# A transformer layer with retrieved experts: 344 dense tokens in place of 352, three slot groups for the gathered ones, and a gate table read four blocks at a time

## The reference

```
q = (x @ w_query) per head, two halves          # 8 heads
s = q . sub_keys                                # 2 x 128 scores per head
top 16 of each half, then top 16 of the 256 sums -> 16 experts per head, 128 per token
g = softmax(top scores)                         # one gate per expert
hid = gelu(x . u_tab[expert])                   # u_tab, v_tab: 16384 x 2048
out = sum over experts of g * hid * v_tab[expert]
```

## Time and profile before

| | before |
|---|---|
| median of 3 runs | 3497.88 us |
| the profiled execution's own time | 3498.18 us |
| its span | 3496.4 us |
| TensorE busy | 3327.0 us, 95% |
| VectorE busy | 2788.3 us, 80% |
| ScalarE busy | 998.9 us, 29% |
| GpSimd busy | 1131.7 us, 32% |
| moved by DMA | 897.01 MB, mean 257 GB/s |

### The profile page before, as it was taken

How to read it: one execution, slowest core, us unless ns; L and a number is a source line. 1 busy time by engine, 2 the same in 40 slices (tenths; PEclk the granted TensorE clock), 3 DMA queues, 4 the chain that set the end, 5 groups by cost and what they waited for, 6 DMA issues and landing times.

```text
span 3496.4 us, 48435 instructions
## 1 busy us (share of the span) xinstructions
PE 3327.0 (95%) x19321; PEld 3047.2 (87%) x19321; DVE 2788.3 (80%) x3985; ACT 998.9 (29%) x1240; POOL 1131.7 (32%) x568
## 2 busy tenths in 40 slices
PE   7999999996898999889999999999999999999996
PEld 2688888886896447889999999999999999999996
DVE  6888888888676668977887787787678878878776
ACT  2322222223223002433333323323323322332222
POOL 2443333333350577002332322233123323333220
PEclk9999999998998999999999999999999999999998
DMA  9644444443556212458989889988788988999895
GB/s 401 240 160 165 160 156 159 159 165 133 206 178 258 105 60 73 171 204 299 336 337 347 329 334 340 337 330 335 261 321 326 339 329 324 341 336 328 329 352 201
DMA packets 199241, 897.01 MB, mean 257 GB/s; under 512 B 81893, under 2 KB 82702, under 8 KB 108430
## 3 DMA queue, kind: packets, MB, share of 16 engines
q1 hardware_dynamic: 152974, 558.82, 43.9%
q0 software_dynamic: 46080, 335.56, 25.0%
HBM read 858.03 MB, written 35.21 MB: 255 GB/s over the span
## 4 chain that ended last, share of the span: by engine, by line
PE 79%; DVE 12%; issue 4%; DMA 3%; POOL 2%; ACT 1%; SPq 0%; DVEq 0%; ACTq 0%; POOLq 0%
PE ps_all L987 17%; PE ps_all L1047 9%; PE ps_all L1053 9%; PE ps_all L1048 9%; PE ps_all L994 8%; PE ps_all L952 6%; PE ps_all L714 5%; PE ps_all L716 5%; PE ps_all L715 5%; DVE sb_hot L1897 2%; PE ps_all L660 1%; DVE sb_hot L1893 1%; DVE sb_tops L1626 1%; DVE sb_arena L1630 1%; DMA sb_raw_ring<-in_v_t 1%
## 5 line engine op out<-in xcount | busy, mean ns | idle before, releaser
L1342 ACT ACTIVATE sb_raw_hi<-sb_raw_ring 128x2048 fp32r<-128x2048 f32 x256 | 490.8, 1918 | 1215.8 <-DMA sb_raw_ring<-in_v_t 535.9
L1047 PE MATMUL ps_all<-sb_w_hi,sb_raw_hi 128*128 128x352 f32 x2048 | 658.1, 324 | 20.3 <-DVE sb_w_lo L1916 13.6
L987 PE MATMUL ps_all<-sb_h_hi,sb_raw_hi 128*128 128x352 f32 x2048 | 662.9, 326 | 5.9 <-issue 5.9
L1821 DVE TENSOR_TENSOR sb_raw_lo<-sb_raw_ring,sb_raw_hi 128x2048 fp32r<-128x2048 f32 x256 | 586.5, 2291 | 98.7 <-ACT sb_raw_hi L1342 98.4
L987 PE MATMUL ps_all<-sb_h_lo,sb_raw_hi 128*128 128x352 f32 x2048 | 661.0, 324 | 0.0
L1048 PE MATMUL ps_all<-sb_w_lo,sb_raw_hi 128*128 128x352 f32 x2048 | 656.6, 322 | 0.0
L2086 POOL DMA_INDIRECT sb_gather_ring<-in_u_tab,sb_kept x160 | 267.6, 1673 | 829.8 <-DVE sb_kept L1936 623.6
L2086 POOL DMA_INDIRECT sb_gather_ring<-in_v_tab,sb_kept x160 | 281.4, 1759 | 670.3 <-DVE sb_acc_a L1948 467.5
L1047 PEld LDWEIGHTS ps_all<-sb_w_hi,sb_raw_hi 128*128 128x128 f32 x2048 | 386.1, 189 | 21.9 <-issue 20.2
L2012 POOL TENSOR_TENSOR sb_w_low<-sb_w_raw,sb_w_high 128x2048 fp32r<-128x2048 f32 (+1 forms) x64 | 265.4, 4146 | 427.2 <-ACT sb_w_high L1153 427.2
L987 PEld LDWEIGHTS ps_all<-sb_h_hi,sb_raw_hi 128*128 128x128 f32 x2048 | 387.8, 189 | 6.7 <-issue 6.7
(11 more groups left out here) (270 smaller groups left out, 5608.3 us busy)
## 6 DMA issues: line engine op xcount, KB each, us to landing
sb_raw_ring<-in_u_t SPq DMA_DIRECT2D x128, 1024.0 KB
sb_raw_ring<-in_v_t SPq DMA_DIRECT2D x128, 1024.0 KB
sb_arena<-in_ada_wt SPq DMA_DIRECT2D x96, 512.0 KB, 4.3
sb_w_raw<-in_w_t SPq DMA_DIRECT2D x32, 1024.0 KB, 5.0
sb_w_raw<-in_w_v SPq DMA_DIRECT2D x32, 768.0 KB, 4.1
sb_g_ring<-table_scratch SPq DMA_DIRECT2D x64, 352.0 KB
sb_arena<-in_ada_w SPq DMA_DIRECT2D x10, 2048.0 KB, 11.8
table_scratch<-sb_stage SPq DMA_DIRECT2D x7, 2816.0 KB, 8.7
```

The costliest lines, as they stand in the source:

```text
L987: last = mm(acc, raw_hi[:, r[0], kk * P:(kk + 1) * P], part[:, kk, :], start=i == 0, stop=False)
L1047: mm(accs[c], v, w_hi[:, slots[e], :], start=e == 0, stop=False)
L1342: acti(raw_hi[:, k % 2, :], raw_ring[:, k % RAW, :], ACT.Copy).then_inc(S["un_hi"], 1)
L1821: vec.tensor_tensor(raw_lo[:, k % RAW, :], raw_ring[:, k % RAW, :], raw_hi[:, k % 2, :].bitcast(f32), ALU.subtract)\
```

## The change

The dense tokens become 344 (XT = 40), cut into 8 stages of 43. A stage has ten groups of 4 tokens and one of 3. The gate table is read four blocks at a time (`QUAD`), each row piece 172 numbers long. The last 40 tokens stand three times over the partitions (120 rows used), in groups of 43, 43 and 42 slots; their 43 transfers still fetch 128 rows, the last 8 by an index cleared to 0, and VectorE works on 120. `DOTS` is 171 per table. The third part of `y_t` has 88 tokens; its banks are cleared by a matmul with zeros, the tokens come in by matmuls with the unit matrix, and the three groups by `pick_x`, all added up in the same banks. The small tiles that are kept over the stage are placed elsewhere.

```diff
-XT = 32
+XT = 40
 XG = P // XT
+XP = XG * XT
 ND = T - P - XT
-XSLOTS = SLOTS // XG
+XSLOTS = -(-SLOTS // XG)
-NGROUP = ND // GROUP
-STAGE = 44
+STAGE = 43
-PER_STAGE = STAGE // GROUP
+PER_STAGE = -(-STAGE // GROUP)
+NGROUP = NSTAGE * PER_STAGE
+QUAD = 4
 def slot_at(n):
-    m, j = n // 5, n % 5
-    return (True, 4 * m + j) if j < 4 else (False, SLOTS + m)
+    m, j = n // 4, n % 4
+    return (True, 3 * m + j) if j < 3 and n < DOTS - 1 else (False, SLOTS + m)
+def group_at(n):
+    c = n % PER_STAGE * GROUP
+    return n // PER_STAGE, c, min(GROUP, STAGE - c)
...
-        g_ring = placed("g_ring", at, [P, 2, NSTAGE, 2 * STAGE])
+        g_ring = placed("g_ring", at, [P, 2, NSTAGE, QUAD * STAGE])
...
+            def g_load(q):
+                if QUAD * q in QUARTERS:
+                    sp.wait_ge(S[f"g_quarter{QUARTERS.index(QUAD * q)}"], 16)
+                wait(sp, "gated", QUAD * (q - 1))
+                sp.dma_start(g_ring[:, q % 2, :, :], g_d[:, :, QUAD * q * STAGE:QUAD * (q + 1) * STAGE].rearrange("n j c -> j n c"))\
+                    .then_inc(S[f"g_in{q % 2}"], 16)
...
-            for p in range(2):
-                g_load(p)
+            g_load(0)
+            g_load(1)
             stage_store(NSTAGE - 1, (1, 2, 3))
             g_load(2)
             next_load(EARLY - 2)
-            for p in range(3, 5):
-                g_load(p)
             for k in range(EARLY - 1, UNITS):
                 next_load(k)
-                if k in (14, 17, 19, 22):
-                    g_load((14, 17, 19, 22).index(k) + 5)
-                if kind == "up" and n >= EARLY and n % 2 and n + 3 < NKEYS:
-                    g_load((n + 3) // 2)
+                if k in (EARLY - 1, EARLY + 5):
+                    g_load((EARLY - 1, EARLY + 5).index(k) + 3)
+                if kind == "up" and n >= EARLY and n % QUAD == QUAD - 1 and n + 1 + QUAD < NKEYS:
+                    g_load((n + 1) // QUAD + 1)
...
                 if t == 2:
                     pe.wait_ge(S["zs"], 2)
                     pe.wait_ge(S["sq_done"], 2)
                     pe.wait_ge(S["pick_x"], 1)
+                    zeros, any_rows = pick_x[:, 0:1].to_broadcast([P, P]), ident[:, :].unsqueeze(1).to_broadcast([P, 4, P])
+                    for b in range(4):
+                        mm(psum[:, y0 + b * NB:y0 + (b + 1) * NB], zeros, any_rows, start=True, stop=False)
+                        for kk in range(4 * b, 4 * b + 4):
+                            mm(psum[0:n, y0 + kk * P:y0 + (kk + 1) * P], y_t[:, kk, at:at + n], ident[:, :], start=False, stop=False)
                     pe.wait_ge(S["gr_used"], 2 * DOTS)
                     for b in range(4):
-                        last = mm(psum[n:P, y0 + b * NB:y0 + (b + 1) * NB], pick_x, acc_x[:, b * NB:(b + 1) * NB], start=True, stop=True)
+                        last = mm(psum[:, y0 + b * NB:y0 + (b + 1) * NB], pick_x[0:XP, :], acc_x[0:XP, b * NB:(b + 1) * NB], start=False, stop=True)
...
+            link(vec.tensor_scalar(gates_x, iota[:, 0:XSLOTS], 0.0, None, ALU.mult))
+            vec.tensor_copy(eidx_x, gates_x)
             vec.tensor_copy(eidx_a, pair_id[:, 0, :])
             vec.tensor_copy(eidx_last, pair_id[:, 1, :]).then_inc(S["g_fin"], 1)
...
+            link(vec.tensor_scalar(pick_x, ident[:, :], 0.0, None, ALU.mult))
+            vec.tensor_reduce(pick_x[:, P - XT:P], ident[:, 0:XP].rearrange("p (a j) -> p j a", a=XG), axis=AX, op=ALU.add)\
+                .then_inc(S["pick_x"], 1)
```

More of the change, by code:

```diff
@@ L249, in build_program @@
         hid_all = take(DOTS)
-        pick_x = take(XT)
-        at = SM + D
         raw_hi = rounded("raw_hi", at, [P, 2, D])
@@ L257, in build_program @@
         stage = [placed(f"stage{n}", a, [P, NKEYS, STAGE]) for n, a in enumerate((at, M0))]
-        take = carver(placed("route_b", at, [P, 7 * D // 2]))
+        pick_x = placed("pick_x", at + 2 * (S8 + 2) * ND, [P, P])[:, :]
+        take = carver(placed("route_b", at, [P, 2 * (S8 + 2) * ND]))
         qt_sb = take(2 * T).rearrange("p (m t) -> p m t", m=2)
@@ L605, in _ @@
             for a in range(XG):
-                part, cols_ = slice(a * XT, (a + 1) * XT), slice(a * XSLOTS, (a + 1) * XSLOTS)
-                sp.dma_start(eidx_x[part, :], eidx_last[P - XT:P, cols_]).then_inc(S["xe_in"], 16)
-                sp.dma_start(gates_x[part, :], gates[P - XT:P, NT - 1, cols_]).then_inc(S["xe_in"], 16)
+                first, end = a * XSLOTS, min((a + 1) * XSLOTS, SLOTS)
+                part, place, slots = slice(a * XT, (a + 1) * XT), slice(0, end - first), slice(first, end)
+                sp.dma_start(eidx_x[part, place], eidx_last[P - XT:P, slots]).then_inc(S["xe_in"], 16)
+                sp.dma_start(gates_x[part, place], gates[P - XT:P, NT - 1, slots]).then_inc(S["xe_in"], 16)
             next_load(PRE - 1)
@@ L1026, in _ @@
                 wait(pe, "g_ev", n - 3)
-                for x in range(GROUP):
+                for x in range(group_at(n)[2]):
                     last = mm(bank(4 + n % 4)[:, x * P:(x + 1) * P], hot[:, n % 4, 1, x, :], hot[:, n % 4, 0, x, :],
@@ L1355, in table_out @@
             def table_out(n):
-                if n % PER_STAGE == 0:
-                    wait(act, f"g_out{n // PER_STAGE % 2}", 16 * (n // PER_STAGE // 2))
+                s, c, g = group_at(n)
+                if c == 0:
+                    wait(act, f"g_out{s % 2}", 16 * (s // 2))
                 wait(act, "g_mm", n + 1)
-                c = n % PER_STAGE * GROUP
-                acti(stage[n // PER_STAGE % 2][:, :, c:c + GROUP], bank(4 + n % 4).rearrange("p (x i) -> p i x", x=GROUP), ACT.Copy)\
+                acti(stage[s % 2][:, :, c:c + g], bank(4 + n % 4)[:, 0:g * NKEYS].rearrange("p (x i) -> p i x", x=g), ACT.Copy)\
                     .then_inc(S["g_ev"], 1)
@@ L1891, in _ @@
                 wait(dve, "g_mm", n - 3)
-                shape = [P, GROUP, NKEYS]
-                vec.tensor_tensor(hot[:, n % 4, 0, :, :], iota[:, :].unsqueeze(1).to_broadcast(shape),
-                                  by_slot[:, 0, n * GROUP:(n + 1) * GROUP].unsqueeze(2).to_broadcast(shape), ALU.is_equal)
-                for x in range(GROUP):
-                    c = n * GROUP + x
-                    last = vec.tensor_scalar(hot[:, n % 4, 1, x, :], iota[:, :], by_slot[:, 1, c:c + 1], by_slot[:, 2, c:c + 1],
-                                             ALU.is_equal, ALU.mult)
+                s, c, g = group_at(n)
+                c += s * STAGE
+                shape = [P, g, NKEYS]
+                vec.tensor_tensor(hot[:, n % 4, 0, 0:g, :], iota[:, :].unsqueeze(1).to_broadcast(shape),
+                                  by_slot[:, 0, c:c + g].unsqueeze(2).to_broadcast(shape), ALU.is_equal)
+                for x in range(g):
+                    last = vec.tensor_scalar(hot[:, n % 4, 1, x, :], iota[:, :], by_slot[:, 1, c + x:c + x + 1],
+                                             by_slot[:, 2, c + x:c + x + 1], ALU.is_equal, ALU.mult)
                 last.then_inc(S["g_hot"], 1)
```

48 lines of the change are left out of this document (22 added, 26 removed).

## The result

The changed kernel takes 3475.8 us, the median of four runs (3469.04 to 3480.21), against 3498.1 us (3495.89 to 3499.47) for the kernel before on the same chip. The ratio is 0.9935, with a 95% interval of 0.9918 to 0.9952. That is 22.3 us less, where 32 were forecast; the range held it. The profiled execution was the fastest of the four: 3469.04 us, span 3467.0.

The account below looks back on a forecast made before the run. TensorE was taken to bound the dense expert stage, 53% of the span. Terms -38.6 - 3 + 0.4 + 2 + 4 + 3.4 = -31.8 us took 3498.2 to 3466 us; low end 3456, high end 3482.

Parts of the forecast that it names:

- Dense columns: Dense expert stage: matmuls of 344 columns start every 156.7 ns, 3.33 ns sooner, over 11568 matmuls: -38.6 us.
- The rival that columns come in larger steps: Dense stage: 344 columns are paid as 352, so no gain there; 3501 us, chance 0.03.
- Table: Table stage on VectorE: eight groups have 3 tokens and take less time, -3 us (bounds -3.3 and -1).
- Clears: Before the table: clearing gates_x and eidx_x on VectorE's path costs +0.4 us (0.3 to 0.6).
- Switch: From table to first down unit: larger four-block table loads go ahead of the stores, +2 us (0 to +4).
- Gathers at the 15 turns: Where up blocks give way to down groups: more gathers make later landings into waits, +4 us (0 to +15).
- the rival that the turns eat the gain: The 15 turns each cost 2.4 us beyond their slack, cancelling 36 us; 3498 us, chance 0.03.
- Tail: Last 128 rows: clears and true fp32 products lengthen TensorE's work before the last tile, +3.4 us (1.5 to 12).
- the dense stage loses fewer than 25 us: The prediction's own sign of failure: a dense stage shortened by less than 25 us makes it wrong.
- The ring ceiling: Up stretches: DMA rings cannot exceed the 346 GB/s seen, so units take 8.01 us; 3514 us, chance 0.03.
- The milder latency: DMA rings in up stretches: latency grows without a ceiling, costing 12 to 25 us; 3474 to 3487 us, chance 0.14.
- my own case: The forecast itself, whole kernel: 3466 us, its own range 3456 to 3478, chance 0.76.

Follow-up runs that it names:

- the second trace: The changed kernel run again without edits: its second profiled execution, 3481.56 us.
- e4: Changed kernel with 160 gathers per table instead of 171, so the last 40 tokens are incomplete: 3469.71 us, ratio 0.9907 to the kernel before.
- The second set: The changed kernel run again without edits, beside the kernel before: median 3478.66 us over six runs, ratio 0.9935.

## Why the prediction was right, and where it was off

*Dense columns, the mis-sized term.* Forecast: 156.7 ns and 3.33 ns saved. Measured: 157.4 in up and 157.65 in down units, against 160.48 and 160.36, so 2.9 ns, and 11568 of them give -33.4 us, not -38.6. The fit was checked on a window of counted matmuls: 61.9 us over 387 gives 160.0, but two of these reach in from before, and 385 starts give 160.5. For 256 columns the prediction did leave out the two that the edges cut. So the fit was not exact to 0.1 ns: 352 columns already lay 0.4 to 0.5 ns above its line, and 344 lie 0.7 to 1.0 above it. The distance and place of the rows explain up to 2.5 us of the missing 5. What makes the rest isn't known. The rival that columns come in larger steps is out.

*Table.* -3 forecast, 3.3 measured. *Clears.* +0.4 forecast; the first table operation came 1.0 us sooner in the trace after and 1.3 in the second, so they can't be seen.

*Switch.* +2 (0 to 4) forecast; +0.4 and +1.7 in two traces of the changed kernel, and two blocks in place of four take 1.4 to 3.5 off. Right in kind, about 1 in size.

*Gathers at the 15 turns.* The size was +4, and the place was wrong. The unchanged kernel less e4's leaves 9 us, inside the 0 to 15 given. Before, the largest wait at the first 14 turns was 0.8 us; after, the largest were 0.6 and 1.0 in the two traces. So the rival that the turns eat the gain is out too. What grew are landings of raw rows, above all in front of unit 251, where five transfers of 1 MB lie ahead, and in the second trace at scattered units. I had also read the 4.63 us of the earlier trace rows as a sign of the turns' latency. It is no such thing: the last part of the order has seven up units ahead of its down units, so that no unit lies between the block whose low part is wanted and the first down unit. Gelu, gate and low part stand bare there. In the trace after, `sb_w_lo` runs from 3354.1 to 3354.6 and TensorE starts 0.1 us behind it; the row says "issue", but the low part is what came last. The wait is 3.3 to 5.5 us in the rows shown and 3.3 to 5.8 in all traces but the one with 120 rows, whatever the edit.

*Tail.* +3.4 forecast, 3.8 and 4.4 measured. TensorE and VectorE after (answering to the earlier trace rows):

```profile
3440.66 2.07 PE L1093 MATMUL ps_all<-sb_ident,sb_pick_x 128*128 128x512 f32 x2 [11.85 <-DVE sb_raw_ring L2018]
3442.53 1.92 PE L1095 MATMUL ps_all<-sb_ident,sb_y_t 128*88 128x128 f32 x8
...
3446.73 1.02 PE L1093 MATMUL ps_all<-sb_ident,sb_pick_x 128*128 128x512 f32 x2
...
3450.20 3.60 PE L1098 MATMUL ps_all<-sb_acc_x,sb_pick_x 120*128 120x512 f32 x8
...
3455.89 2.29 DVE L2018 TENSOR_TENSOR sb_raw_ring<-ps_all,sb_gate_sb 128x2048 f32<-128x2048 f32 x1 [3.95 <-ACT sb_gather_ring L1437]
```

The first clear and the first eight products take twice the time of the later ones (2.07 against 1.02), as the half-speed start was priced, and VectorE stands 3.95 us before its last tile.

*The sum.* From the median: -33.4 - 3.3 - 1 + 1 + 9 + 4 = -23.7, measured -22.3. The main term came 5 us short and the late landings cost 5 more than taken; the two together are the 10 us between forecast and median. The 9 is the difference of two medians. The traces have for it what waits and slow stretches took beyond the pace: 5 us more than before in the fast execution and 16 more in the second, with the 9 between them.

*By its own signs.* The prediction calls itself wrong if the dense stage loses fewer than 25 us. It lost 29.2 us in the first profiled execution and 18.3 in the second, so one passes this test and the other does not, and the kernel's usual time lies between the two. TensorE's waits were 16.7 and 23.6 us, the first inside the 13 to 20 and the second above. The matmuls, the rings' share (0.96) and the gap before the last tile came as said or nearly so. The mechanism held; what it leaves for late landings was too little.

*The rivals.* The ring ceiling would have needed a stop at 346 GB/s; the rings ran at 368 for 100 us without a wait of TensorE. The Trainium skill (DMA: Bandwidth & Descriptors, Where 436 GB/s comes from) has about 358 GB/s for one core; this trace disagrees by 10 GB/s. The milder latency, given 0.14, was the nearest of them: the median lies in its range (3474 to 3487), and in my own case's too (3456 to 3478). The second set's median, 3478.7, lies in the former alone. Its mechanism was at work, with 9 us by the medians and not 12 to 25, though the slower of the two traces, with 16, would lie in that; the rest of the distance is the pace.

## What to carry to other kernels

Where TensorE is the bound, check the pace of a matmul size by the mean distance of starts and not by a window's count: the count hid that 352 columns already lay off the fitted line, and 344, a size that no row had shown, lay further off. An error of 0.4 ns in a saving of 3.3 was 5 us here. A wait that stands in one row is a sign of the place it stands in; look up what the order of work does there before it is taken for a sample of all such places. And transfers that nobody is in a hurry for belong one by one between the urgent ones: five issued in a row cost 3 to 6 us at one unit once the rings were fuller, 1 to 2 before. A wait of TensorE is to be priced with the half-speed stretch that can follow it.

## What the runs showed of the hardware

Gathers of 120 rows took some 1.7 times the ring time of gathers of 128 (578 ns a row for 335) and, as 86 of 342, made the kernel 3% slower, for less data. The rings held 368 GB/s for 100 us under unbroken matmuls. The matmuls of this kind were paced at 120.0 ns for 256 columns and 226.7 for 512, but for 344 columns 0.7 to 1.0 ns above the line through these, and 0.1 to 0.3 of it goes with the distance of the rows, 1376 bytes against 1408, or with their place. At each new pass of the loop in its program (at about 2080, 2445 and 2812 us in the changed kernel, in front of units 81, 129 and 177) TensorE stood for 1.1 to 3.9 us in every trace with gathers of 128 rows, mostly in rows that end in "issue". Why isn't known. Behind some waits of 1.9 to 5.8 us the granted clock was 0.50 for some microseconds and the matmuls started 287 ns apart; behind others of up to 3.3 us it stayed at 1.00.
